# Combined inputs rounded one tile later in the tails, and the fourth feed-forward stage's made behind the second mixer's tails

## The reference, cut to what matters

```
x = x + 0.5 * (silu(norm(x) @ w_gate) * (norm(x) @ w_up)) @ w_out      # inner width 2816
norm(x) = x * rsqrt(mean(x * x) + 1e-6) * g
```

## Time and profile before

| what | value |
|---|---|
| median of three runs | 2039.19 us (2037.29 to 2039.55) |
| the profiled execution | 2039.16 us |
| its span, first to last instruction | 2037.1 us |
| PE busy | 2013.0 us (99%) |
| DVE, POOL, ACT busy | 1275.8, 1129.1, 1064.0 us |
| granted TensorE clock, mean | 0.997 |

### The profile page before, as it was taken

One profiled execution on the slowest core, in us unless ns is written; L12 is line 12 of the kernel. 1 busy time (PEld: TensorE's weight loads), 2 busy tenths in 40 slices (PEclk: granted clock), 3 DMA queues, 4 the chain that ended last, 5 costly groups with the idle time before them and its releaser, 6 DMA issues. The chain is left out here.

```text
span 2037.1 us, 33284 instructions
## 1 busy us (share of the span) xinstructions
PE 2013.0 (99%) x12322; PEld 1768.2 (87%) x12322; DVE 1275.8 (63%) x2245; ACT 1064.0 (52%) x1764; POOL 1129.1 (55%) x936
## 2 busy tenths in 40 slices
PE   9999999999999999999998999999999998999999
PEld 7998998777778879989987998998878877998997
DVE  7752765767763577626767763664688867742762
ACT  6642653444433456525655652554677755642651
POOL 2764875443333448756755775775323335764873
PEclk9999999999999999999999999999999999999999
DMA  4232333422221223332232333233444422332322
GB/s 170 99 104 90 113 97 113 146 73 73 70 66 62 94 80 108 109 109 94 92 106 74 114 104 104 95 102 115 115 135 128 125 93 73 105 111 86 105 99 97
DMA packets 69087, 206.19 MB, mean 101 GB/s; under 512 B 8448, under 2 KB 9472, under 8 KB 68928
## 3 DMA queue, kind: packets, MB, share of 16 engines
q1 hardware_dynamic: 67520, 201.29, 30.7%
q10 hardware_dynamic: 1408, 2.78, 0.4%
HBM read 189.49 MB, written 2.10 MB: 94 GB/s over the span
## 5 line engine op out<-in xcount | busy, mean ns | idle before, releaser
L624 POOL TENSOR_TENSOR w_lo<-raw,w_hi 128x512 fp32r<-128x512 f32 (+2 forms) x464 | 523.5, 1155 | 657.9 <-ACT w_hi L1255 496.4
L1255 ACT ACTIVATE w_hi<-raw 128x512 fp32r<-128x512 f32 (+2 forms) x472 | 359.0, 765 | 319.0 <-PE ps L701 252.0
L636 POOL TENSOR_TENSOR w_lo<-s,w_hi 128x512 fp32r<-128x512 f32 x234 | 312.7, 1338 | 195.9 <-ACT w_hi L1255 194.9
L777 PE MATMUL ps<-t_hi,w_hi 128*128 128x256 f32 x1248 | 355.3, 285 | 8.7 <-POOL w_lo L636 5.0
L778 PE MATMUL ps<-t_lo,w_hi 128*128 128x256 f32 x1248 | 354.6, 284 | 0.0
L779 PE MATMUL ps<-t_hi,w_lo 128*128 128x256 f32 x1248 | 354.5, 284 | 0.0
L636 POOL TENSOR_TENSOR w_lo<-raw,w_hi 128x512 fp32r<-128x512 f32 x234 | 304.7, 1317 | 39.6 <-ACT w_hi L1255 39.4
L699 PE MATMUL ps<-xn_hi,w_hi 128*128 128x512 f32 x648 | 260.1, 401 | 9.5 <-POOL w_lo L624 7.5
L777 PE MATMUL ps<-xn_hi,w_hi 128*128 128x256 f32 x936 | 265.1, 283 | 0.0
L778 PE MATMUL ps<-xn_lo,w_hi 128*128 128x256 f32 x936 | 264.9, 283 | 0.0
L779 PE MATMUL ps<-xn_hi,w_lo 128*128 128x256 f32 x936 | 264.9, 283 | 0.0
(11 more groups left out here) (260 smaller groups left out, 3760.5 us busy)
## 6 DMA issues: line engine op xcount, KB each, us to landing
raw<-weights SPq DMA_DIRECT2D x294, 512.0 KB, 3.3
raw<-weights SPq DMA_DIRECT2D x68, 256.0 KB, 2.8
raw<-weights SPq DMA_DIRECT2D x32, 384.0 KB, 3.0
k_hi_twice<-sb_k_hi SPq DMA_DIRECT2D x31, 128.0 KB, 2.3
k_lo_twice<-sb_k_lo SPq DMA_DIRECT2D x31, 128.0 KB, 2.3
x_sb<-x_t SPq DMA_DIRECT2D x8, 256.0 KB, 5.9
bias<-rel ACTq DMA_DIRECT2D x1, 2048.0 KB, 10.0
q_both<-sb_q_hi SPq DMA_DIRECT2D x16, 128.0 KB, 2.2
```

The source lines that it names most:

```text
L624: last = nc.gpsimd.tensor_tensor(w_lo[s][:, k, :], raw[s][:, k, :], w_hi[s][:, k, :].bitcast(F32), ALU.subtract)
L636: nc.gpsimd.tensor_tensor(quad_of(n, i, w_lo), factor(n, F, i, raw, s_sum), quad_of(n, i, w_hi).bitcast(F32), ALU.subtract).then_inc(S["q_ ...
L777: pe.matmul(to, w[0][:, k, :], hi, start=opens, stop=False, skip_group_check=True)
L1255: return nc.scalar.activation(dst, src, ACT.Copy)
```

## The change

Four things are moved, and no arithmetic is added or taken away.

- **Tails in front of stages 2 and 3:** ACT rounds piece k - 1 in tile k (from tile 1 on) and DVE splits piece k - 2, each a tile later than before. `round_input` and `square` of a tile thus no longer have a rounding behind them that waits for DVE's work of the same tile.
- **Tails in front of stage 4:** t1 is neither made nor rounded nor split in them (`make_xg` stays). All of stage 4's combined inputs are made behind the tails, in `plain_tiles`.
- **Start of stages 2, 3 and 4:** on ACT the rounding of the fourth unit (`ahead(u + 1)`) and of the combined inputs left over stands in front of `first_norm`, where it stood behind. Product 5's weights are rounded in front of `copy_a`. The mean's two matmuls (in stage 3 four) stand one tile earlier (`MEAN_AT` = 1).
- **Start of stage 1:** ACT rounds product 1's weights and does `copy_c` between the second and the third piece of t2 to t4; DVE does `sum_1` and `sum_3` after the first piece's split, `sum_2` after the last; product 5's weights are rounded in front of `copy_a` and `round_h`.

```diff
@@ plain_tiles, ACT
                 for k in range(QUAD):
                     if k == 2:
                         silu(0, 2)
+                        round_7(0, PLAIN[0], 1)
+                        copy_c(0, PLAIN[0])
                     round_t(0, k)
+                round_7(0, PLAIN[0], 5)
+                copy_a(0, PLAIN[0])
                 round_h(0, 2)
-                round_7(0, PLAIN[0], 1)
-                copy_c(0, PLAIN[0])
-                copy_a(0, PLAIN[0])
-                for i in (5, 6, 2):
-                    round_7(0, PLAIN[0], i)
+                round_7(0, PLAIN[0], 6)
+                round_7(0, PLAIN[0], 2)
                 silu(0, 3)
                 round_h(0, 3)
                 return
             u = FFN_BASE[n]
             round_sums(FFN_STAT[n])
             ahead(u)
+            ahead(u + 1)
+            if n == 3:
+                for k in range(QUAD):
+                    round_t1(n, k)
+            for j in range(T_IN_TAIL[n], QUAD):
+                round_t(n, j)
             first_norm(FFN_STAT[n])
-            ahead(u + 1)
             if n == 2:
                 second_norm()
-            for j in range(T_IN_TAIL[n], QUAD):
-                round_t(n, j)
             F = PLAIN[n]
             round_7(n, F, 1)
             copy_c(n, F)
             silu(n, 0)
+            round_7(n, F, 5)
             copy_a(n, F)
-            round_7(n, F, 5)
             round_h(n, 0)
@@ tail, ACT
                 if k < QUAD:
                     make_xg(m, k)
-                    round_t1(m, k)
-                elif k < QUAD + T_IN_TAIL[m]:
-                    round_t(m, k - QUAD)
+                if 1 <= k <= QUAD and m < 3:
+                    round_t1(m, k - 1)
+                elif QUAD < k <= QUAD + T_IN_TAIL[m]:
+                    round_t(m, k - QUAD - 1)
@@ tail, DVE
-                if k < QUAD:
+                if k < QUAD and m < 3:
                     make_t1(m, k)
-                elif k < QUAD + T_IN_TAIL[m]:
+                elif QUAD <= k < QUAD + T_IN_TAIL[m]:
                     make_t(m, k - QUAD)
-                if 1 <= k <= QUAD:
-                    split_t1(m, k - 1)
-                elif QUAD < k <= QUAD + T_IN_TAIL[m]:
-                    split_t(m, k - QUAD - 1)
+                if 2 <= k <= QUAD + 1 and m < 3:
+                    split_t1(m, k - 2)
+                elif QUAD + 1 < k <= QUAD + 1 + T_IN_TAIL[m]:
+                    split_t(m, k - QUAD - 2)
@@ plain_tiles, DVE
                 split_both(0)
+                sum_1(0, PLAIN[0])
+                sum_3(0, PLAIN[0])
                 split_both(1)
                 plain_h(0, 2)
                 split_both(2)
                 split_both(3)
+                sum_2(0, PLAIN[0])
                 split_h(0, 2)
+                rest_of_6(0, PLAIN[0])
+                plain_gate(0, 3)
+                plain_h(0, 3)
+                split_h(0, 3)
             else:
                 split_sums(FFN_STAT[n])
+                if n == 3:
+                    for k in range(QUAD):
+                        make_t1(n, k)
                 for j in range(T_IN_TAIL[n], QUAD):
                     make_t(n, j)
+                if n == 3:
+                    for k in range(QUAD):
+                        split_t1(n, k)
...
-                return
-            sums_of_first(n, 0)
-            rest_of_6(n, PLAIN[n])
-            plain_gate(n, PLAIN[n] - 1)
-            plain_h(n, PLAIN[n] - 1)
-            split_h(n, PLAIN[n] - 1)
@@
-MEAN_AT = 2
+MEAN_AT = 1
```

## The result

The changed kernel takes 2025.49 us, the median of four runs (2025.26 to 2025.77), against 2039.18 us (2037.29 to 2039.55, four runs): a ratio of 0.9935, with a 95% interval of 0.9918 to 0.9952. It is 13.7 us faster; forecast were 2025.6 us and a range of 2020.5 to 2031.5. Beside the later runs the kernel before had medians of 2038.84, 2038.03 and 2038.45 us, so about 1 us of the 13.7 depends on which of its executions one compares with. Two executions of 5685.93 us (f_round1_early) and 7740.52 us (the kernel before, beside v3), about three and four times as long as all others, are left out.

The account below looks back on a forecast made before the run. TensorE bounds the kernel, with 18.2 us idle at the four stage starts. Stage terms -0.1 - 4.4 - 4.2 - 4.9 = -13.6 us against 2039.16 give 2025.6 us, range 2020.5 to 2031.5.

Parts of the forecast that it names:

- Stage 2: Start of stage 2: TensorE's waits go, gate ends at 746.7, TensorE itself decides; -4.4 us, ends -4.5 and -2.4.
- Stage 3: Start of stage 3: faster tail and shorter Ln-to-gate chain bring product 7 earlier; -4.2 us, ends -1.7 and -7.3.
- Stage 4: Start of stage 4: waits go without t1 in the tail, gate ends at 1700.7; -4.9 us, ends -2.5 and -10.
- the one of product 1's weights 1.2: Stage 4's start: POOL's operation on product 1's weights adds 1.2 us to DVE's list.
- DVE keeps its run: Rival, stages 3, 4: DVE runs back to back, POOL waits; gates 2.5 and 3.6 us earlier, 2019.5 us; chance 0.10.
- Stage 1: Stage 1's start: product 5's wait goes (-1.1), two POOL operations in the way (+1.0); -0.1 us, ends -1.3 and +0.5.
- G + 11.8: Stages 2 to 4: product 7 starts 11.8 us after G, the first DVE gate's end, unless TensorE gets there later.
- The clock will fall there again for 3.4 us: Stage 4's start: TensorE reaches product 5 about 3 us early, clock falls for 3.4 us, the chain outlasting its cost.
- Tails no faster: Rival: DVE in the tails trades one wait for another; stages 3 and 4 give 1.7 and 2.5, 2030.9 us; chance 0.15.
- the clock outlasts the chain: Rival: clock stays at 1.2 GHz beyond the chain in stages 3 and 4; 2027.3 us for one, 2029.0 for two; chance 0.10.
- slower: Rival: TensorE stays at 1.2 GHz after the starts; 2043 us; chance 0.03.
- no effect: Rival: starts are bound by something the trace hides, such as a late transfer; within 4 us of 2039; chance 0.05.

Follow-up runs that it names:

- f_round1_early: Changed kernel with product 1's weights rounded in front of first_norm instead of behind it, in stage 4 alone; 2025.80 us.
- v3: Changed kernel with stage 1's old order, stage 4's t1 in the tail, norms and splits moved in stages 3 and 4, second gate behind sum_3 everywhere; 2017.06 us.
- a_tails_undone: Changed kernel with the tails before stages 2 and 3 undone: ACT rounds piece k in tile k, DVE splits piece k - 1; 2028.83 us.
- c_norm_first: Changed kernel with the first norm on ACT again in front of ahead(u + 1) and the roundings of the combined inputs; 2030.93 us.
- d_small_undone: Changed kernel with MEAN_AT = 2, product 5's rounding behind copy_a in stages 2 to 4, and stage 1's old order; 2024.99 us.
- b_t1_in_tail: Changed kernel with stage 4's t1 made, rounded and split in the tails again, roundings and splits a tile later; 2024.90 us.
- c2_norm_between: Changed kernel with first_norm on ACT behind ahead(u + 1) (in stage 4 behind t1's roundings) but before the roundings of t2 to t4; 2024.93 us.
- e_no_rests: Changed kernel with POOL's rest of stages 3 and 4's third and fourth units cut to 4 of 128 columns, a price measurement only; 2017.80 us.

## Where the prediction was right and where it wasn't

**Stage 2 (-4.4, measured -4.42).** The steps that were given numbers held. Put back by the 0.91 us that the kernel is late there, Ln starts at 744.73 (744.6 was worked out), the gate ends at 746.79 (746.7), and TensorE itself is the later one.

**Stage 3 (-4.2, measured -3.71).** The place and the mechanism held (a_tails_undone). Put forward by 3.51 us, the last update starts at 1081.1 (1080.2), the last piece is there at 1094.4 (1094.1), Ln starts at 1095.2 (1094.8), and from Ln to the gate it takes 5.84 us (5.8). So the term was 0.5 us too large by DVE's tail: the update came 0.9 us later than worked out, and about half of that is left at the gate. But the reason given for the second half was not complete. c_norm_first has the same stage 3 as the changed kernel in the old order: with the norm in front the chain behind Ln is longer, and Ln is earlier by as much. Of the 3.7 us, 2.5 are the tails'; the other 1.2 go with none of the parts that were undone singly (c_norm_first -0.06, d_small_undone -0.12), and their cause stays open.

**Stage 4 (-4.9, measured -6.12).** Put forward by 7.22 us, the tail ends at 1682.7 (1682.8), make_t at 1694.0 (1694.1), Ln starts at 1694.8 (1695.0). Then DVE is through at 1698.8 where 1700.1 was worked out. The step that failed is "the one of product 1's weights 1.2": POOL's operation took no turn between DVE's splits, as f_round1_early confirmed. This is the rival "DVE keeps its run", true for the row of splits and false for make_t1 and the first of make_t, where four of DVE's operations took 1.5 us instead of 0.48. It came true for one operation in five, and gave 1.2 of the 3.6 us that it would have given in full. The Trainium skill's rule cited there ("SBUF — State Buffer", "Who interferes with whom") gives the pair of ports to one engine for the whole of one instruction. Where the engines take turns (1.51 to 1.57 us for DVE's operations) the trace agrees with it; that POOL's operation waited through several instructions of DVE (3.25 us at 1689.53) is more than the rule says, and no run here tells which rows alternate.

Of these 6.12 us the parts undone singly account for 2.6 (c_norm_first); undoing the others cost stage 4 nothing. The remaining 3.5 us are by elimination those of the tail, whose roundings no longer wait for DVE's work of the same tile; that is argued and not shown.

Also, t1's way out of the tail was credited with the waits on ACT that "go, since t1 is no longer made in the tail". The wait of TensorE behind them is gone with the later rounding alone (b_t1_in_tail).

**Stage 1 (-0.1, measured +0.28).** The step that failed is "+1.0 for two POOL operations in the way". Each cost about 1.0 on its own, an operation of make_t 1.40 instead of 0.42 and a split 2.04 instead of 0.95. Timeline of the changed kernel, DVE:

```profile
43.11 1.40 DVE L2124 TENSOR_TENSOR t_raw<-t_raw,xg 128x256 f32<-128x256 f32 x1
...
47.69 2.04 DVE L2132 TENSOR_TENSOR t_lo<-t_raw,t_hi 128x768 fp32r<-128x768 f32 x1
```

Together 2.07 us, against 1.08 for the wait gone. That the stage lost only 0.3 is due to a move that the term left out: `split_h` of tile 2 (0.67 us) now stands behind `sum_2`, so `sum_2` starts 0.3 us later (52.66, less the 0.63 of the late start, for 51.73). Here rounding the weights early freed nothing, since POOL then took their rest while DVE worked on two sources in SBUF.

**The constant chain.** G + 11.8 was right to 0.02 us in both stages that it decides, and it takes 11.78 to 11.80 us in every trace with product 5 in front of `copy_a` in which a chain and not TensorE was the later one. It is what made the sum come out.

**The clock.** "The clock will fall there again for 3.4 us" was wrong in the profiled execution: product 5 of stage 4 waited 1.59 us, not about 3, and the clock stayed at 2.4 GHz, as it did behind 2.00 us in stage 3. The other three executions have a mean granted clock of 0.999 instead of 1.000, so a fall may well be in them; they took 2025.26 to 2025.67 us against 2025.77, so it cost nothing, as said. But the falls of the kernel before were not free either. Among the eight executions of it that ran beside the first four experiments, four had a mean granted clock of 0.997 and took 2039.25 to 2039.88 us, and four had 0.998 or 0.999 and took 2037.33 to 2038.43. Among the fourteen beside the later runs, five had 0.997 and took 2038.81 to 2039.53, nine had 0.999 and took 2037.20 to 2038.08, but for one of 2039.06. The likely reason is the fall near 1684: it lies in front of the mean's matmuls, and Ln waited for them. By this some 1.5 us of the 13.7 may go with the falls, which no run shows by itself, and the prediction had them inside G's new place without saying so.

**The signs.** Idle time at the four starts was 2.60, 0.00, 4.37 and 3.96 us, where 2 to 2.5, near 0, about 4 and about 5 were named, and the gate of stage 2 came 5.3 us earlier counted from before's clock (5 to 6 named). Of the two signs of being wrong the first stayed away: product 7 of stage 2 waits for nothing. The second came, by a hair: the last update in front of stage 3 starts at 1077.56, 1.55 us after its product ended (1075.62 + 0.39), where more than 1.5 was to count as wrong. It was 5.5 us before the change, so the mechanism stands. But the tail was not freed as far as worked out: DVE works without a gap from 1074.81 on, through the previous tile's squares, rests and split (L2132 at 1076.69), and the update had to wait for that.

**Rivals.** "Tails no faster" is refuted by a_tails_undone, "the clock outlasts the chain" and "slower" by the windows at 1.00, "no effect" by the result.

## What to carry to other kernels

When an engine's list waits for another engine's work of the same step, let it take that work one step later before moving the work elsewhere: in two stages the shift gave 0.8 and 2.5 us, and in the third, moving the work out was 0.5 us worse than the shift. A norm or another long wait should stand at the place in its engine's list where its input arrives: too early it blocks what is ready, too late it waits behind what is not, and by the traces here the right place differs from stage to stage of one kernel. And before an off-path engine is given its work earlier, look at which operations of the busier one it will then meet.

## What the runs showed of the hardware

**A row of splits shuts POOL out, make_t doesn't.** Both are DVE operations with two sources in SBUF. Beside make_t (L2121 to L2126) and make_t1, POOL and DVE took turns in every trace: DVE's operations rose from 0.42 to 0.48 us to 1.36 to 1.63, and POOL's from 1.30 to about 1.5. Beside four splits in a row (L2132), POOL's single operation took 3.25 us in the changed kernel, a_tails_undone and d_small_undone, 4.49 in f_round1_early, 4.30 in c2_norm_between and 3.04 in e_no_rests, and DVE lost nothing. In the kernel before and in c_norm_first the same splits did alternate (three and one of the four in stage 4); there POOL had been working when DVE's splits began, those of t1 included. It had been idle for 6.87 to 8.11 us in front of the six, and for 1.96 us or less where it got in between two splits. Whether either decides is open: no run here parts them from each other or from the length of the operations (beside make_t1 in the changed kernel POOL had been idle for 5.68 us and got every turn).

**A wait's length alone doesn't decide the clock's fall.** TensorE in d_small_undone, stages 3 and 4, and the granted clock (fourth column) behind each:

```profile
1102.01 0.39 PE L777 MATMUL ps<-t_hi,w_hi 128*128 128x256 f32 x1 [2.52 <-POOL w_lo L636]
...
1696.62 0.39 PE L777 MATMUL ps<-t_hi,w_hi 128*128 128x256 f32 x1 [2.11 <-POOL w_lo L636]
```

```profile
1697.62:1701.03 3.41, 3.41 (x18) 0.50 0.02 5
1100.00:1106.00 6.00, 3.58 (x27) 1.00 0.00 1
```

After 2.52 us the clock stayed at 1.00, after 2.11 us it fell to 0.50 for 3.41 us, and in the changed kernel neither 2.00 nor 1.59 us brought it down, while in the kernel before it fell (0.51 from 1110.98 to 1114.39) behind a wait of only 1.94 us at 1109.98. A fall is thus not to be counted on, nor its absence, from one wait in a trace.
